# Scan stages of a seven-layer forward pass: level copies on ScalarE, one inverse root, joined gate weights, turned rows inside units

## The reference

```python
def gla_chunk_scan(q, k, v, log_f):            # hgrn: one-sided decay
    G = jnp.cumsum(log_f)                      # in chunks of 64
    o_inter = (q * exp(G)) @ state
    attn = einsum(q, k, where(causal, exp(G_t - G_s), 0)); o_intra = attn @ v
    state = exp(G_last) * state + (k * exp(G_last - G)).T @ v
# gla: the same with decay exp(-|L_t - L_s|), 4 heads of 128 x 256
o = rms_norm(o, gain)                          # hgrn: per head of 128
y = o * silu(gate)                             # then y @ w_out
```

## Time and profile before

| | us |
|---|---|
| median of 3 runs | 2056.19 (2055.5 to 2057.44) |
| the profiled execution, its own time | 2057.1 |
| its span, first to last instruction | 2055.3 |
| TensorE busy | 1908.8, 93% |
| VectorE busy | 1207.5, 59% |
| ScalarE busy | 910.0, 44% |
| GpSimd busy | 593.1, 29% (MLPs only) |
| mean granted TensorE clock | 0.973 of full |

### The profile page before, as it was taken

One profiled execution on the slowest core, in us unless ns is written; L12 is line 12 of the kernel. 1 busy time (PEld: TensorE's weight loads), 2 busy tenths in 40 slices (PEclk: granted clock), 3 DMA queues, 4 the chain that ended last, 5 costly groups with the idle time before them and its releaser, 6 DMA issues.

```text
span 2055.3 us, 27371 instructions
## 1 busy us (share of the span) xinstructions
PE 1908.8 (93%) x11072; PEld 1678.5 (82%) x11072; DVE 1207.5 (59%) x2062; ACT 910.0 (44%) x981; POOL 593.1 (29%) x132
## 2 busy tenths in 40 slices
PE   6899989989888988999989999999999988989998
PEld 5688877779777877899778899889899977779996
DVE  6788787775977397332566522566522376863236
ACT  5555545345443343444354444443444434334442
POOL 0000000000000001787400688500487700037870
PEclk9999999999899999999999999999999999999999
DMA  7344434534332234455443455444655533164551
GB/s 291 123 145 143 178 130 144 195 142 150 103 124 97 110 117 155 164 198 190 145 162 137 182 179 192 183 156 163 221 180 188 186 124 140 62 222 171 189 199 44
DMA packets 53412, 324.94 MB, mean 158 GB/s; under 512 B 8480, under 2 KB 11936, under 8 KB 16064
## 3 DMA queue, kind: packets, MB, share of 16 engines
q1 hardware_dynamic: 45344, 310.10, 41.4%
q10 hardware_dynamic: 7968, 13.44, 2.0%
HBM read 322.47 MB, written 1.05 MB: 157 GB/s over the span
## 4 chain that ended last, share of the span: by engine, by line
PE 73%; DVE 20%; ACT 4%; issue 2%; DMA 0%; SPq 0%; DVEq 0%; ACTq 0%
PE project L908 41%; PE output L908 25%; DVE wlo L1563 3%; PE turn L1084 1%; ACT whi L1256 1%; DVE XTl L2049 1%; PE output L1026 1%; PE output L1049 1%; DVE arena L1675 1%; DVE tok L2257 1%; DVE arena L1901 1%; DVE arena L1903 1%; DVE arena L1927 1%; ACT XTh L1376 1%; PE turn L1005 1%
## 5 line engine op out<-in xcount | busy, mean ns | idle before, releaser
L876 POOL TENSOR_TENSOR wlo<-raw,whi 128x2048 fp32r<-128x2048 f32 x128 | 592.9, 4660 | 1415.0 <-ACT whi L1256 1398.1
L1256 ACT ACTIVATE whi<-raw 128x2048 fp32r<-128x2048 f32 x291 | 554.4, 1913 | 477.3 <-PE project L908 308.4
L908 PE MATMUL project<-XTh,whi 128*128 128x256 f32 x1488 | 427.0, 287 | 4.4 <-DVE XTl L2049 3.0
L908 PE MATMUL project<-XTh,wlo 128*128 128x256 f32 x1488 | 425.0, 286 | 0.0
L908 PE MATMUL project<-XTl,whi 128*128 128x256 f32 x1488 | 424.9, 286 | 0.0
L2285 DVE TENSOR_TENSOR arena<-arena 128x512 f32<-128x512 f32 x64 | 143.2, 2271 | 462.0 <-ACT arena L1513 462.0
L1563 DVE TENSOR_TENSOR wlo<-raw,whi 128x2048 fp32r<-128x2048 f32 x163 | 376.6, 2323 | 39.0 <-ACT whi L1256 38.7
L908 PE MATMUL output<-whi,YTh 128*128 128x512 f32 x736 | 291.7, 396 | 13.2 <-DVE YTl L2049 11.4
L908 PEld LDWEIGHTS project<-XTh,whi 128*128 128x128 f32 x1488 | 290.0, 195 | 7.4 <-DVE XTl L2049 4.9
L908 PEld LDWEIGHTS project<-XTh,wlo 128*128 128x128 f32 x1488 | 289.9, 195 | 1.0
L908 PEld LDWEIGHTS project<-XTl,whi 128*128 128x128 f32 x1488 | 289.6, 195 | 0.0
(11 more groups left out here) (245 smaller groups left out, 2104.7 us busy)
## 6 DMA issues: line engine op xcount, KB each, us to landing
raw<-in_units SPq DMA_DIRECT2D x291, 1024.0 KB, 4.8
arena<-in_ln_g ACTq DMA_DIRECT2D x8, 512.0 KB, 4.1
arena<-in_ln_b ACTq DMA_DIRECT2D x8, 512.0 KB, 4.9
arena<-in_mem_norm_gain ACTq DMA_DIRECT2D x2, 512.0 KB, 4.9
tok<-in_mem SPq DMA_DIRECT2D x2, 512.0 KB, 5.7
xres<-in_x SPq DMA_DIRECT2D x1, 1024.0 KB, 12.9
arena<-in_mem ACTq DMA_DIRECT2D x1, 1024.0 KB, 6.6
arena<-in_p ACTq DMA_DIRECT2D x4, 256.0 KB, 4.3
```

What stands on the lines that cost most here:

```text
L876: pool.tensor_tensor(wlo[:, slot, :], raw[:, slot, :], whi[:, slot, :], ALU.subtract).then_inc(lo_pool, 1)
L908: mm = pe.matmul(out, x if x_stationary else w, w if x_stationary else x, start=start and i == 0, stop=stop and i == 2, skip_group_check=True)
L1256: act.activation(whi[:, slot, :], raw[:, slot, :], ACT.Copy).then_inc(hi_done, 1)
```

## The change

- ScalarE takes over the copies of levels 6, 7 and 8 (and level 0 in gla) out of PSUM. It copies rectangular cells instead of masked whole tiles; what lies outside is zeroed once in gla by a memset on VectorE.
- For level 8 ScalarE reads the logs where they are, so that VectorE's copy L1923 goes. The two gla products L1901 and L1903 become one instruction of 2048 columns.
- The step that told TensorE that q and k are there (L1891) becomes a step `z0` of its own, earlier in the list; gla's level 0 no longer waits for VectorE at all.
- In `oscan`, gate, norm gain and 0.5 are multiplied together first; in gla both row tiles share one inverse root; the scaling by the root writes y and replaces `ymul` (in gla for the first half of the columns; the other half keeps it).
- hgrn's `f` and `fq`, gla's gate and the vtok unit have their `ahead` parts at other places; the mem part of y is multiplied and turned earlier; in the second hgrn scan the three cover units stand at levels 1, 3, 5 instead of 2, 4, 6.
- The rows y of the first half are turned between the two banks of gla's last gate unit; the tail of `w_out_b` is cut in three pieces with the turns of x between them, and x's last turn stands inside gla's first projection.

```diff
@@ plan()
-        if tag in ("qk", "fq"):
-            add("ahead", n=m, on="sv")
+        if tag in ("qk", "fq", "f"):
+            add("ahead", n=m, on=behind_post)
...
-        at = [int((i + 1) * every) for i in range(len(cover))]
+        at = [int((i + 1) * every) - pp for i in range(len(cover))]
...
     project(wb, 0, "fq", feature_major=True, scale=1.0, hg=0, second=0,
-            between=lambda: add("fgate", hg=0, part=0, gf=gf, heads=len(heads)))
+            between=lambda: (drain(), add("ymul", chunk=2, layer=1, second=0),
+                             add("fgate", hg=0, part=0, gf=gf, heads=len(heads))))
     add("fgate", hg=0, part=1)
-    drain()
-    add("ymul", chunk=2, layer=1, second=0)
+    add("z0", gq=n["pd"])
     n["vtok"], c1 = cover_of(wb, 2048 + 512, "vtok", c=1)
-    c1[0]()
     for h in range(H2):
         turn("y", h, 2, "Y", 8)
+    c1[0]()
     levels("hgrn", 0, c1[1:] + cover_of(wb, 3584, "gate", buf="y", gh=0)[1])
-    add("ymul", chunk=0, layer=1, second=0)
...
-    tail(2)
-    add("qpost", g=g, post="resid", src_n=n["src"])
-    turn_x(pre="q_evac")
+    add("tail", work=tuple((x, u) for x in range(3) for u in range(2)), ahead=False, **last)
+    add("ahead", n=last["n"], on="sv")
+    add("qpost", g=g, post="resid", xs=(0, 1, 2), src_n=n["src"])
+    turn("x", 0, 0, "X", 0, pre="q_evac")
+    turn("x", 0, 1, "X", 4, pre="q_evac", late=True)
+    add("tail", work=((3, 0),), ahead=False, **last)
+    turn("x", 1, 0, "X", 0, pre="q_evac")
+    add("tail", work=((3, 1),), ahead=False, **last)
...
         levels("gla", 0, cv + cg)
-        add("ymul", chunk=0, layer=0, second=1)
-        project(w, 2560, "gate", buf="G", gh=1)
-        for h in range(H2):
-            turn("y", h, 0, "Y", 0)
+        _, one, scalar_post, _ = pieces(w, 2560, "gate", buf="G", gh=1)
+        one(0)
+        one(1, ahead="s", between=[lambda h=h: turn("y", h, 0, "Y", 0) for h in range(H2)])
+        add("ahead", n=len(units) - 1, on="v")
+        scalar_post()
@@ ScalarE: level l runs the exponential, then the copy of level l-1
+                if l == 8:
+                    moves = [(AT[:, :, 2, :], banks[0][:, :].rearrange("p (j t) -> p j t", j=4))]
+                elif l == 7:
+                    moves = [(AT[0:64, :, 0:2, 64:128], compact[0:64])]
+                elif l == 6 and not g:
+                    moves = [(AT[64 * n:64 * n + 32, :, 0:2, 64 * n + 32:64 * n + 64],
+                              compact[64 * n:64 * n + 32, :, :, 32 * n:32 * n + 32]) for n in range(2)]
+                elif l == 6:
+                    moves = [(AT[32 * n:32 * n + 32, 2 * b:2 * b + 2, 0:2, 32 * (n ^ 1):32 * (n ^ 1) + 32],
+                              both[b][32 * n:32 * n + 32, :, :, 32 * (n ^ 1):32 * (n ^ 1) + 32])
+                             for b in range(2) for n in range(4)]
+                else:
+                    moves = [(AT[64 * n:64 * n + 64, 2 * b:2 * b + 2, 0:2, 64 * n:64 * n + 64],
+                              both[b][64 * n:64 * n + 64, :, :, 64 * n:64 * n + 64]) for b in range(2) for n in range(2)]
+                for dst, src in moves[:-1]:
+                    act.activation(dst, src, ACT.Copy).then_inc(act_own, 1)
+                act.activation(*moves[-1], ACT.Copy).then_inc(lev_evac, 1)
...
+                            act.activation(Dv[:, :, 1, :], Gv[:, :, 1, :], ACT.Exp, scale=s).then_inc(act_own, 1)
+                            ins = act.activation(Dv[:, :, 0, :], Dv[:, :, 0, :], ACT.Exp, scale=s)
+                        evacuate(f, l - 1, f["L"] - 1)
@@ ScalarE and VectorE, post of glagate
+                    ahead(f["m"])
@@ VectorE
-                    dve.tensor_tensor(QE[l % 2], q, Dx, ALU.mult).then_inc(dve_own, 1)
-                    dve.tensor_tensor(KE[l % 2], k, Dx, ALU.mult).then_inc(z_ready, 1)
+                    dve.tensor_tensor(both, ar(24, 2048).rearrange("p (a b) -> p a b", a=2),
+                                      Dx.unsqueeze(1).to_broadcast([P, 2, 1024]), ALU.mult).then_inc(z_ready, 1)
...
+                    for h in range(H2):
+                        gs = gsG[0][:, h, :] if g else yA[:, h, f["hg"] * 512:f["hg"] * 512 + 512]
+                        dve.scalar_tensor_tensor(out=gs, in0=gs, scalar=0.5, in1=gain.unsqueeze(1).to_broadcast([P, n, w]),
+                                                 op0=ALU.mult, op1=ALU.mult).then_inc(dve_own, 1)
...
                         dve.wait_ge(a2v, nth("a2v"))
                         dve.wait_ge(a2v, nth("a2v"))
+                        dve.tensor_reduce(st[:, 16 + ng * r:16 + ng * r + ng], sq.rearrange("p (a b) -> p a b", a=ng), AX_X,
+                                          ALU.add).then_inc(dve_own, 1)
...
+                    dve.tensor_scalar(st[:, 16:24], st[:, 16:24], 1.0 / w, EPS, ALU.mult, ALU.add).then_inc(dve_own, 1)
+                    rsqrt(st[:, 24:32], st[:, 16:24], st[:, 80:88])
```

More of the change, by code:

```diff
@@ L115, in unit @@
         m = len(units) - 1
-        add(step, n=m, ahead=ahead and not hold[0], **f)
+        add(step, n=m, ahead=False if hold[0] else ahead, **f)
         if hold[0]:
@@ L173, in project @@
             between()
-        one(1, ahead=tag not in ("qk", "fq"), between=[turn_first] if early else ())
+        one(1, ahead=tag not in ("qk", "fq", "f"), between=[turn_first] if early else ())
         fields = scalar_post()
@@ L215, in begin_output, with one @@
         conv = w[0] == "conv_w_out"
-        def one(u, first=False):
-            unit("out", (w, "Q", u, 0), g=g, u=u, first=first, src=src, conv=conv, heads=len(heads))
+        def one(u, first=False, scan=0):
+            unit("out", (w, "Q", u, 0), g=g, u=u, first=first, scan=scan, src=src, conv=conv, heads=len(heads))
         def tail(u):
@@ L228, in output @@
         g, one, tail = begin_output(w, 1024, src)
-        one(0, first=True)
+        one(0, first=True, scan=w[1] + 1 if w[0] == "gla_w_out" else 0)
         flush()
@@ L377, in turn_y0 @@
             turn("y", h, 0, "Y", 0)
-    project(wb, 512, "fq", feature_major=True, scale=1.0, hg=1, second=0,
-            between=lambda: (turn_y0(), add("fgate", hg=1, part=0, gf=gf, heads=len(heads))))
+    project(wb, 512, "fq", feature_major=True, scale=1.0, hg=1, second=0, behind_post="s",
+            between=lambda: (turn_y0(), add("ahead", n=len(units), on="v"),
+                             add("fgate", hg=1, part=0, gf=gf, heads=len(heads))))
     add("fgate", hg=1, part=1)
-    c1 = cover_of(wb, 3584 + 512, "gate", buf="y", gh=1)[1]
-    c1[0]()
-    c1[1]()
+    add("z0", gq=n["pd"])
+    _, one, scalar_post, _ = pieces(wb, 3584 + 512, "gate", buf="y", gh=1)
+    one(0)
+    one(1, ahead="s")
+    behind.append(lambda m=len(units) - 1: add("ahead", n=m, on="v"))
+    scalar_post()
     g, one, tail = begin_output(("w_out_b", 0), 1536)
     levels("hgrn", 1, [lambda: one(0, first=True), lambda: one(1), lambda: one(4)], pp=True)
-    add("ymul", chunk=1, layer=1, second=0)
     one(5)
@@ L399, in gla, with fill @@
         w = ("gla_w_in", j)
-        project(w, 0, "fq", feature_major=True, scale=SCALE, second=1)
+        def fill():
+            if j == 0:
+                (turn("x", 1, 1, "X", 4, pre="q_evac", late=True))
+        project(w, 0, "fq", feature_major=True, scale=SCALE, second=1, between=fill)
         add("glrsplit", j=j)
@@ L1385, in _ @@
                 elif kind == "tail":
-                    if not f["ple"]:
+                    if not f["ple"] and f["ahead"]:
                         ahead(f["n"])
@@ L2152, in _ @@
                     last.other(glr_ready, f["j"] + 1)
+                elif kind == "z0":
+                    for b in range(2):
+                        dve.wait_ge(p_evac[b], f["gq"])
+                    dve.wait_ge(*last.at)
+                    dve.tensor_copy(st[:, 92:93], st[:, 93:94]).then_inc(z_ready, 1)
+                    last.other(z_ready, nth("z"))
                 elif kind == "lev":
```

140 lines of the change are left out of this document (89 added, 51 removed).

## The result

The changed kernel takes 2032.96 us in the median (2031.76 to 2033.85, 4 runs) against 2056.82 (2055.5 to 2057.9, 4 runs) for the kernel before on the same chip: ratio 0.9884, 95% interval 0.9867 to 0.9901. That is 1.2% faster. The forecast was 2034. The profiled span (first to last instruction of one execution) fell from 2055.3 to 2031.7, by 23.6, of which the forecast had 22.5.

A forecast was written before the change was run, and what follows sets the result against it. TensorE, busy 1908.8 of 2055.3 us, bounds the kernel, so only its idle time or lower clock can pay. Gains of -29.7 at full clock and +7.2 coming back net -22.5, giving 2034; range 2024 to 2047.

The forecast's parts named there:

- B: Second hgrn scan: levels -3.6, waits behind -1.3; clock losses +0.9 at level 2's new gap, +2.0 for uncovered levels 5 to 8.
- Start and end of A: First hgrn scan: level 1 earlier, -1.3; ScalarE's level copies delay the end, +1.0; wait behind the scan gone, -1.35.
- A's clock: First hgrn scan: TensorE idles 5 us ahead of level 1, so level 1 and its unit run slow, +1.5.
- rival 3: Slower: the low clock takes each new gap, 3.2 at worst, slower than before from the eleventh drop; 2062, chance 0.04.
- The cut tail and the first gla projection: Between hgrn and gla: low-part gaps vanish but one returns, -0.6; slow projection clock gone, -1.5; clock loss back, +0.6.
- Levels of C and D: Two gla scans: VectorE's chain earlier, gaps 1.2, 2.3, 2.2 at levels 2, 4, 6; -4.9 each, +1.1 clock loss.
- gaps of 2.2 cost 1.8 a drop in 0.6 of cases: Gla scans: gaps of 2.2 bring the low clock, 0.6 x 1.8 each, +2.2 over both scans.
- Behind the product: Behind both gla scans: y ready sooner, gap of 4.31 gone, -3.8, and -1.8 for the low clock; -5.6 each.
- ScalarE's small copies: Gla level 6: eight copies at 0.2 us each, 1.6 in all; bounds 0.20 and 0.6 each.
- Rival 1: The clock stays full, so none of the 7.2 us clock loss comes back; 2027, chance 0.20.
- Rival 2: Only what follows the scans pays; the levels keep their pace as ScalarE's copies delay other work; 2042, chance 0.16.
- Rival 4: The moved steps only exchange waits, a late whi or wlo for each gap closed; 2056, chance 0.03.

The follow-up runs named there:

- turns_behind: Changed kernel with the rows y of gla's first half turned behind the whole last gate unit, not between its two banks; 2037.86 us, ratio 0.9911.
- gla_wlo_back: Changed kernel with the ahead parts of gla's vtok and gate units put back behind their posts; 2037.81 us, ratio 0.9913.
- cover_246: Changed kernel with the three cover units of the second hgrn scan at levels 2, 4, 6 again; 2039.89 us, ratio 0.9920.
- old_norm: Changed kernel with gla's work behind the product as before: root per row tile, no joined gate, ymul for the first half; 2034.82 us, ratio 0.9897.
- hgrn67_dve: Changed kernel with the copies of levels 6 and 7 of both hgrn scans on VectorE again; 2029.86 us, ratio 0.9876.
- tail_whole: Changed kernel with the hgrn output tail uncut and all turns of x ahead of gla's first projection; 2037.17 us, ratio 0.9904.
- copies_dve: Changed kernel with all of ScalarE's level copies (0, 6, 7, 8) done by VectorE again; 2035.73 us, ratio 0.9898.
- a_wlo_late_67: Changed kernel with the first hgrn scan's first vtok wlo behind its first levels, and hgrn level 6 and 7 copies on VectorE; 2025.68 us, ratio 0.9855.
- two_roots: Changed kernel with an inverse root for each of the two row tiles in gla; 2032.84 us, ratio 0.9888.
- gla_zwait: Changed kernel with TensorE's level 0 of the gla scans waiting for VectorE's z step again; 2033.52 us, ratio 0.9890.
- a_wlo_late: Changed kernel with the wlo of the first hgrn scan's first vtok unit issued behind its first levels; 2032.93 us, ratio 0.9887.

## Why the prediction was right, step by step

**What bounds the kernel.** Right. Of the 23.6 of span, 3.1 is busy time of TensorE and 20.5 idle time, and the gaps that closed were ended by VectorE; turns_behind, gla_wlo_back, cover_246 and old_norm each put a part of it back by the order of the steps or by VectorE's work, with the matmuls unchanged.

**The total.** It was met to 1.1 of span, but the misses of its eleven stages add up to 6.6: A came out 1.9 longer than forecast, B and D's levels 0.4 each, the other eight shorter by up to 0.9. That the sum came so near is in part luck.

**Start and end of A** (-1.3, +1.0, -1.35 behind it). Right as waits: level 1 came 1.5 earlier, level 8 1.1 later, the stall behind f is gone with 1.6. hgrn67_dve confirms the middle one as the price of ScalarE's copies ahead of tanh and exponential. The mis-sized term is A's clock: +1.5 in the forecast, and level 1 with its unit took 3.68 and 7.94, 3.9 more than at full clock (2.0 and 5.7). The worst drop known was rival 3's, of 3.2; I had taken half of it without a row that says half.

**B** (-3.6, -1.3, +0.9, +2.0). The gap of 2.29 at level 2 and the slow stretch at 645 came as said, at 1.7 and about 2.1. cover_246 shows what was not in the forecast: that the early cover is needed because level 0 comes early; without it the gap would be 5.0. The forecast's +2.0 for uncovered levels is a matter of the clock and not of the cover alone: hgrn67_dve has the same levels uncovered and no slow stretch behind them.

**The cut tail and the first gla projection** (-0.6, -1.5, +0.6). Measured -2.05, and tail_whole puts back 2.0. Right. But the low clock that is gone there appeared in the vtok unit, 1.6.

**Levels of C and D** (-4.9, +1.1). The forecast had level 0 to 2, 2 to 4, 4 to 6 and 6 to the product at 10.6, 11.7, 11.8 and 12.0; C measured 10.1, 11.6, 11.6 and 11.4, D 11.2, 11.6, 11.6 and 13.0. The gaps 1.2, 2.3, 2.2 were 0.84, 2.29, 0.70 in C and 1.91, 2.32, 2.30 in D. The wait for the last copies ahead of the product is 1.18, from 767.7 to 769.0 in the forecast. C's 11.4 is a full clock at level 6, D's 13.0 the low one. The reason given for part of it holds only in part: I credited 1.3 to ScalarE's diagonal, and copies_dve shows that it is there at level 2 and lost again at the end of D, by a slow level 6. And "gaps of 2.2 cost 1.8 a drop in 0.6 of cases" overlooked that a drop inside the levels costs nothing while VectorE paces them; it costs behind level 6 alone. The size came out near by luck, since D had its drop at level 6 and C had it at level 4: by an estimate from these rows (13.0 against 11.4), the two scans would have been 1.6 longer with both drops at level 6, and 1.6 shorter with both at level 4. How often it drops was near: 29 of 44 behind gaps of 2.15 to 2.48, where I had said 0.6.

**Behind the product** (-3.8, -1.8). Measured -4.4 and -1.7. Turns 1.7 and joined gate with `ymul` gone 1.1 of it are shown, one root at nothing; the remaining 1.6 was not taken apart. Each was put back alone, so that the parts add up is assumed. Here I had counted one root as part of the way to y; it is only a part of VectorE's queue, in front of which VectorE waits anyway.

**ScalarE's small copies** (0.2 each). They come 0.29 apart, inside the bounds of 0.2 and 0.6, with no effect on level 7. The figures of the forecast, 186 ns a call and 93 overlapped, stand in the Trainium skill, "ScalarE: Activation LUTs", section "What ACT_TABLE_LOAD costs"; without the overlap they give an estimated 0.29 for 128 columns. That is the distance measured: between these copies no overlap shows, so the eight take 2.3 and not 1.6. Why, no run here shows. The Trainium skill, "ScalarE: Activation LUTs", Rules for kernel authors, advises VectorE for plain arithmetic. By copies_dve both places are equal in D and ScalarE is the better one in C, by 2.8 with the vtok unit, of which a slow level 6 is 1.6; in hgrn hgrn67_dve finds VectorE the better one by 1.1 ahead of level 8. So in this kernel the queue decides and not the rule.

**Rivals.** Rival 1 (full clock throughout, 2027) did not hold. a_wlo_late_67 comes to 2025.7, with a mean clock of 0.978 against 0.974, and less idle time besides. Rival 3's single price was met and passed at A (3.9 for 3.2), not its number; and by its own figures the tenth drop already gives 2059, more than before the change, where it says the eleventh. Rival 2 fell: D's levels paid 3.4 and C's 4.4. Rival 4 (2056) fell with the total.

**Not foreseen.** The first MLP of gla is 0.9 shorter. All of it lies right behind a gap of 2.7 that both kernels have. TensorE's time line of the kernel before, and a stretch there:

```profile
829.59 1.79 PE L1084 MATMUL turn<-ident,xres 128*128 128x128 f32 x8 [2.71 <-DVE xres L2276]
```

```profile
830.00:835.00 5.00, 4.44 (x21) 3.92 (x20) 1.57 (x3) 3.11 (x3) 4.73 (x2) 0.50 0.31 96
```

The same of the changed kernel:

```profile
816.82 1.32 PE L1107 MATMUL turn<-ident,xres 128*128 128x128 f32 x8 [2.70 <-DVE xres L2364]
```

```profile
817.00:822.00 5.00, 4.24 (x24) 3.77 (x24) 1.78 (x3) 3.10 (x3) 4.49 (x1) 0.74 0.39 109
```

From this turn to the next wait for x 184.5 us passed before and 183.7 now, and the difference is there after the first 24 matmuls (7.4 and 6.5 behind the turn); from then on the two traces run alike. So it is the granted clock and no work that went. two_roots and gla_zwait read 183.7 too, the ten others 184.3 to 184.9. Why the clock came back sooner in three of them is open.

## What to carry to other kernels

- Where one engine has no idle bracket through a loop of stages, add up its instructions for one round: that sum is the pace, and a delay of another engine inside the loop (a slow clock too) is free as long as the wait behind it is longer than the delay. In the gla scans it was; in B, where TensorE waits little behind level 2, a slow level 2 cost its whole length. Gains come from starting that engine's chain earlier or from what follows its last round.
- An edit that helps in its own stage can be given back by the clock in the next. Time edits together as well as alone: two that gave 0.5 and 4.4 of span alone gave 7.8 together (by the means of their executions 0.2, 2.3 and 6.9).
- When an early start closes one gap, look for the next place where the same engine is waited for, and move cover there in the same change; the one without the other was worth less than nothing in B.

## What the runs showed of the hardware

The granted clock after a gap is not set by that gap alone. In the gla scans of these fourteen traces, of the levels that TensorE entered after a wait for VectorE and whose rows are whole, none of 38 was slow after 0.55 to 1.94 us of idle time, 29 of 44 were after 2.15 to 2.48, and 2 of 5 after 2.85 to 3.56 (slow: 2.46 to 3.67 for 2.05). In the second hgrn scan, though, level 8 was slow after 0.41 (1.90 for 1.13), and behind the same gap of 0.95 level 7 took 2.00 in the changed kernel and in hgrn67_dve, 3.15 in a_wlo_late and 3.67 in copies_dve. Which of the gaps of 2.3 is followed by the drop differs between layers: D of the changed kernel has it at level 6, C at level 4. The Trainium skill, "TensorE: Matmul & The Clock Gate", Part 1, has short idle gaps leave the clock up; the rows of 2.15 to 2.48 disagree in 29 of 44 cases. What decides between two equal gaps is not settled here.

A copy of 32 partitions by 128 columns from PSUM takes ScalarE 0.27 with the next one 0.29 later, and one of 256 columns 0.37 and 0.40: halving the columns saves 0.11, not half. (The copies of 128 x 128 from SBUF in the earlier trace rows, busy 0.30, stand 0.20 apart.)
